# Unabsorbed prompt attention, decays of the scan by DMA, and the combine as the end of the expert stage, in one decoder layer

## The chip, the cores and the metric

The kernel runs on one core of one Trainium2 chip. The metric is the device time of one execution in microseconds. Before the change three runs gave 2944.58, 2940.27 and 2940.48, a median of 2940.48.

## The reference, cut to what matters

One decoder layer for a prompt of 512 tokens and 8 sample sequences of 8 tokens, all in float32. Three parts of it matter here.

```
# latent attention, per head h; c and kr are shared by all heads
q_lat = q_nope @ w_kv[:, h, :128].T          # 128 -> 256
s     = (q_lat @ c.T + q_rope @ kr.T) * scale, causal
o     = (softmax(s) @ c) @ w_kv[:, h, 128:]  # 256 -> 128
# chunked scan, per chunk of 128 tokens and head
a_cs     = cumsum(dt * a)
decay_ls = exp(where(causal, a_cs[l] - a_cs[s], -inf))
y_diag   = (C @ B.T * decay_ls * dt) @ x
y_off    = (C @ h_prev) * exp(a_cs);  h = exp(a_cs[-1]) * h + states
y        = rms_norm((y + D * x) * silu(z)) * g
# mixture of experts: top 4 of 32, 576 tokens
out = layer_norm(ALPHA * h + sum_k gate[t, k] * expert_k(h[t])) * g2 + b2
```

## The kernel before, in words

The program is a row of stages. Each stage is a block in which every engine has its own instruction stream, ordered by semaphores, and each ends with a barrier of all engines and a clearing of its semaphores (line 140). Inside a stage the order of work is written out by hand. A matrix product in float32 appears in the trace as two passes (two weight loads, two matmul records); a transpose is one.

`stage_prompt_attention`: 8 heads by 4 query blocks of 128 rows, 32 steps. Block q of a head sees 128(q+1) keys. Step i on TensorE: the scores of i (L402 over two halves of the 256 latent columns, L403 over the 64 rotary ones), the transposes of the probabilities of i-1 (L410), the sum over the latent rows for i-2 (L420, two halves), the value projection of i-3 (L430), and one of four parts of the preparation of the next head: its queries (L375), their absorption into the latent space in two halves (L380), its rotary queries (L386). ScalarE copies each part out (`prep_copy`), takes the exponential (L474), and copies the transposes; VectorE adds the mask (L512), takes the maximum, normalises, and copies the results (L522, L527). The next part waits for the copy of the one before; the scores of a new head wait for all four.

`stage_ssd`: 4 groups of 8 heads by 5 units (four chunks of 128 prompt tokens, and one unit of 64 sample tokens), 20 units. In loop k TensorE does `inputs(k)` (transposes, B C, and L1267, which spreads the running sum of every head over the partitions), `gate(k-1)` (L1280), the transposes of unit k-2, and `outputs(k-1)` (L1292, L1295, L1298). VectorE turns the spread sums into differences (L1490), waits for ScalarE's exponential, multiplies by B C (L1495), waits for `y_ready` of unit k-1 (L1502), and runs the chain of y, the state update and the normalisation. POOL makes three scaled copies of x (L1216). In a sample unit TensorE also turns 8 old states and multiplies them (L1317, L1326), and then makes the new states in 8 products (L1335), whose sum with the aged old ones VectorE forms (L1526) while TensorE waits for a free bank. SP loads and stores; it waits for the stores of the states before it loads the next ones. The first computation (L1429) waits for four loads, the last of which is all 2048 norm gains (`gn`).

`stage_experts` runs 32 experts in a counted loop and then up to 18 overflow items, each behind a branch (L1899), none of them taken in this execution. Each item's rows go to DRAM by an indirect DMA of POOL. `stage_combine` (SP L2147, POOL L2168 and L2170, ACT L2175, DVE L2191 to L2204) is a stage of its own: SP loads the four rows of every token for a tile of 128 tokens (three buffers of 2 MB), VectorE adds them one after another to ALPHA times h, then takes statistics and normalises, and POOL applies gain and bias.

Of the kernel before, what the change touches and what calls it, by code (L numbers as in the profile page):

```python
# [8 lines left out]
F32 = mybir.dt.float32  # L9
# [303 lines left out]
def stage_prompt_attention(nc, io, sb):  # L313

    with ExitStack() as ctx:
# [6 lines left out]
        qn_h = buf("qn_h", [P, T])  # L322
        ql_h = buf("ql_h", [P, 2, 2, SEQ])
# [3 lines left out]
        olT = buf("olT", [P, 2, 2, P])  # L327
# [9 lines left out]
        pt_ready, pt_out, pv_ready, pv_out, o_ready, o_out = (sem(n) for n in ("pt_ready", "pt_out", "pv_ready", "pv_out", "o_ready", "o_out"))  # L337
# [4 lines left out]
        with nc.Block() as block:  # L342
# [6 lines left out]
            def _(pe):  # L349
# [17 lines left out]
                def prep(h, part):  # L367
# [4 lines left out]
                    if part == 0:  # L372
                        for piece, b in ((0, 0), (1, 1)):
                            for k in range(2):
                                mm = pe.matmul(banks[:, b, 0:H2], wq[:, k, h * QH:h * QH + NOPE],  # L375
                                               sb.qnT[:, k, piece * H2:(piece + 1) * H2], start=(k == 0), stop=(k == 1))
                    elif part < 3:
                        r = part - 1
                        for piece in range(2):
                            mm = pe.matmul(banks[:, piece, 0:H2], wkT[:, h, r * P:(r + 1) * P],  # L380
                                           qn_h[:, piece * H2:(piece + 1) * H2], start=True, stop=True)
# [6 lines left out]

                pe.wait_ge(rot_out, NT)
                pe.wait_ge(wk_out, 4)  # L390
                for part in range(4):
                    prep(0, part)
                for i in range(n_steps + 3):
                    if i < n_steps:
# [6 lines left out]
                        for r in range(2):  # L401
                            pe.matmul(o, ql_h[:, h % 2, r, q * P:(q + 1) * P], sb.cT[:, r, 0:n], start=(r == 0), stop=False)  # L402
# [9 lines left out]
                    if 2 <= i <= n_steps + 1:  # L412
                        j = i - 2
                        pe.wait_ge(pt_out, j + 1)
                        if j >= 1:
                            pe.wait_ge(pv_out, j)
                        q = step(j)[1]
                        for r in range(2):
                            for k in range(q + 1):
                                mm = pe.matmul(banks[:, 5, r * P:(r + 1) * P], sb.c_tok[:, k, r * P:(r + 1) * P], probT[:, j % 2, k, :],  # L420
                                               start=(k == 0), stop=(k == q))
                        mm.then_inc(pv_ready, 1)
                    if 3 <= i:
                        j = i - 3
                        h = step(j)[0]
                        pe.wait_ge(pv_out, j + 1)
                        if j >= 1:
                            pe.wait_ge(o_out, j)
                        for r in range(2):
                            mm = pe.matmul(banks[:, 6, 0:P], sb.wkv[:, r, h * 256 + NOPE:(h + 1) * 256], olT[:, j % 2, r, :],  # L430
                                           start=(r == 0), stop=(r == 1))
                        mm.then_inc(o_ready, 1)
# [4 lines left out]
            def _(act):  # L437
                def prep_copy(h, part):
                    m = 4 * h + part
                    act.wait_ge(prep_ready, m + 1)  # L440
                    S1 = SEQ - H2
                    if part == 0:
                        act.activation(qn_h[:, 0:H2], banks[:, 0, 0:H2], ACT.Copy)
                        ins = act.activation(qn_h[:, H2:T], banks[:, 1, 0:H2], ACT.Copy)
                    elif part < 3:
                        r = part - 1
                        if h >= 2:
                            act.wait_ge(scored, 4 * h - 4)
                        act.activation(ql_h[:, h % 2, r, 0:H2], banks[:, 0, 0:H2], ACT.Copy)
                        act.activation(ql_h[:, h % 2, r, H2:SEQ], banks[:, 1, 0:S1], ACT.Copy)  # L450
                        ins = act.activation(sb.qlS[:, r, :, h, :], banks[:, 1, S1:H2].rearrange("p (b t) -> p b t", b=NSEQ), ACT.Copy)
# [4 lines left out]

                for part in range(4):
                    prep_copy(0, part)
# [21 lines left out]
            def _(dve):  # L480
# [19 lines left out]
                for i in range(n_steps + 3):  # L500
# [16 lines left out]
                    if 2 <= i <= n_steps + 1:  # L517
                        j = i - 2
                        dve.wait_ge(pv_ready, j + 1)
                        if j >= 2:  # L520
                            dve.wait_ge(o_ready, j - 1)
                        dve.tensor_copy(olT[:, j % 2, :, :], banks[:, 5, 0:2 * P].rearrange("p (r n) -> p r n", r=2)).then_inc(pv_out, 1)  # L522
                    if 3 <= i:
                        j = i - 3
                        h, q = step(j)
                        dve.wait_ge(o_ready, j + 1)
                        dve.tensor_copy(sb.oT[:, h, q * P:(q + 1) * P], banks[:, 6, 0:P]).then_inc(o_out, 1)  # L527
# [598 lines left out]
def stage_ssd(nc, io, sb):  # L1126

    with ExitStack() as ctx:
# [4 lines left out]
        gn = buf("gn", [P, DI])  # L1133
# [8 lines left out]
        dec = buf("dec", [P, 2, HG, P])  # L1142
# [10 lines left out]
        st_out = buf("st_out", [P, 4, NST])  # L1153
# [18 lines left out]
        with nc.Block() as block:  # L1172
            @block.sync
            def _(sp):
# [3 lines left out]
                for g in range(G):  # L1178
                    if g >= 2:
                        sp.wait_ge(z_ready, NT * (g - 1))  # L1180
# [47 lines left out]
            def _(pe):  # L1228
# [9 lines left out]
                def inputs(k):  # L1238
# [25 lines left out]
                    if k >= 1:  # L1264
                        pe.wait_ge(seg_out, k)
# [1073 lines left out]
```

## Time and profile before

| | us |
|---|---|
| median of 3 runs | 2940.48 |
| profiled execution, its time | 2944.55 |
| its span, first to last instruction | 2942.8 |
| prompt attention, 92.5 to 295.9 | 203.4 |
| scan, 897 to 1313 (with the stores at its end) | 416 |
| experts, 1690 to 2854 | 1164 |
| tail, 2854 to 2942.8 | 88.8 |

All times inside the execution are those of the trace, counted from its first instruction. Where a block of several records is given one duration, that is from its first start to its last end, and the ends of matmuls are modelled: blocks on TensorE overlap a little. The number in brackets behind a row is how long the engine was idle before it, and what released it.

### The profile page before, as it was taken

How to read it: one execution, taken by the hardware profiler on the slowest of the kernel's cores; microseconds unless marked ns; L12 is line 12 of the kernel's file. 1: busy time of each engine (PE TensorE's matmuls, PEld its weight loads, DVE VectorE, ACT ScalarE, POOL GpSimd, SP SyncE). 2: the span in 40 equal slices, each digit the busy share in tenths (PEclk: the TensorE clock that was granted, in tenths of full speed). 3: DMA queues.
4: the chain of work that ended last, by engine and by line, in shares of the span. 5: the costliest groups of instructions: out<-in, count | busy, mean ns of one | idle time of the engine just before them, and what ended most of it. 6: DMA issues, size and time to landing. Idle time of an engine off the chain costs nothing. (4 is left out here: it accounts for less than half of the span.)

```text
span 2942.8 us, 36532 instructions
## 1 busy us (share of the span) xinstructions
PE 2590.7 (88%) x13181; PEld 1970.4 (67%) x13181; DVE 1811.8 (62%) x2324; ACT 1345.9 (46%) x1418; POOL 480.5 (16%) x343
## 2 busy tenths in 40 slices
PE   8699899888996999979976189999999999999970
PEld 5376555588994555538843178888888888888860
DVE  0434344332775456541113389999999999999977
ACT  0233232132333444330001077777777777777750
POOL 0000222000001122100000422222222222222214
PEclk9799999988997999879988599999999999999995
DMA  2100444132213112232222199999999999999964
GB/s 85 60 1 1 183 166 166 61 86 63 87 58 106 51 43 86 61 82 66 58 104 86 21 374 403 380 381 380 378 382 379 380 381 378 382 378 379 378 234 175
DMA packets 240095, 581.16 MB, mean 197 GB/s; under 512 B 25344, under 2 KB 114496, under 8 KB 234816
## 3 DMA queue, kind: packets, MB, share of 16 engines
q1 hardware_dynamic: 221384, 503.17, 47.1%
q0 software_dynamic: 17312, 76.57, 7.0%
q8 instruction: 69, 1.13, 0.2%
q14 instruction: 34, 0.28, 0.0%
q10 hardware_dynamic: 1296, 0.01, 0.0%
HBM read 546.87 MB, written 32.71 MB: 197 GB/s over the span
## 5 line engine op out<-in xcount | busy, mean ns | idle before, releaser
L2085 DVE TENSOR_TENSOR w_lo<-w_raw,w_hi 128x2048 fp32r<-128x2048 f32 x290 | 660.5, 2296 | 67.1 <-ACT w_hi L2042 66.8
L2042 ACT ACTIVATE w_hi<-w_raw 128x2048 fp32r<-128x2048 f32 x290 | 554.3, 1916 | 108.9 <-PE banks L1986 108.8
L1986 PE MATMUL banks<-w_hi,x_hi 128*128 128x512 f32 x1024 | 319.4, 393 | 5.2 <-DVE x_lo L2089 5.2
L1986 PE MATMUL banks<-w_hi,x_lo 128*128 128x512 f32 x1024 | 316.4, 390 | 0.0
L1986 PE MATMUL banks<-w_lo,x_hi 128*128 128x512 f32 x1024 | 316.0, 390 | 0.0
L2085 DVE TENSOR_TENSOR w_lo<-mergedT,w_hi 128x2048 fp32r<-128x2048 f32 x98 | 223.6, 2288 | 46.4 <-ACT w_hi L2042 46.4
L2042 ACT ACTIVATE w_hi<-mergedT 128x2048 fp32r<-128x2048 f32 x98 | 187.6, 1915 | 98.5 <-SPq L1932 63.5
L1986 PEld LDWEIGHTS banks<-w_lo,x_hi 128*128 128x128 f32 x1024 | 192.5, 188 | 40.7
L1986 PEld LDWEIGHTS banks<-w_hi,x_lo 128*128 128x128 f32 x1024 | 192.5, 188 | 40.4
L1986 PEld LDWEIGHTS banks<-w_hi,x_hi 128*128 128x128 f32 x1024 | 190.3, 188 | 43.4 <-issue 5.6
L1958 POOL DMA_INDIRECT y_rows<-xT,to_row x33 | 50.5, 1530 | 866.3 <-ACT xT L2072 866.1
L1986 PE MATMUL banks<-w_hi,h_lo 128*128 128x512 f32 x512 | 158.2, 390 | 0.0
L1986 PE MATMUL banks<-w_lo,h_hi 128*128 128x512 f32 x512 | 158.0, 390 | 0.0
L1986 PE MATMUL banks<-w_hi,h_hi 128*128 128x512 f32 x512 | 158.0, 390 | 0.0
L1280 PE MATMUL banks<-wz,xT 128*128 128x512 f32 (+1 forms) x320 | 141.8, 596 | 0.0
L917 PE MATMUL banks_a<-xbcT,w_br_a 128*128 128x288 f32 x512 | 125.5, 406 | 0.0
L1980 PE MATMUL banks<-const,xT 128*128 128x128 f32 x520 | 68.3, 275 | 58.2 <-DMA xT<-h_rows,from_row 58.2
L917 PEld LDWEIGHTS banks_a<-xbcT,w_br_a 128*128 128x128 f32 x512 | 96.8, 190 | 26.0
L1986 PEld LDWEIGHTS banks<-w_hi,h_hi 128*128 128x128 f32 x512 | 96.1, 188 | 20.6
L1986 PEld LDWEIGHTS banks<-w_hi,h_lo 128*128 128x128 f32 x512 | 96.1, 188 | 20.3
L1986 PEld LDWEIGHTS banks<-w_lo,h_hi 128*128 128x128 f32 x512 | 96.1, 188 | 20.3
L1980 PEld LDWEIGHTS banks<-const,xT 128*128 128x128 f32 x520 | 61.5, 143 | 66.9 <-DMA xT<-h_rows,from_row 58.3
(400 smaller groups left out, 4622.7 us busy)
## 6 DMA issues: line engine op xcount, KB each, us to landing
w_raw<-in_exp_w_gu SPq DMA_DIRECT2D x194, 1024.0 KB, 7.6
w_raw<-in_exp_w_down SPq DMA_DIRECT2D x96, 1024.0 KB, 8.3
mergedT<-in_exp_w_gu SPq DMA_DIRECT2D x66, 1024.0 KB, 8.4
mergedT<-in_exp_w_down SPq DMA_DIRECT2D x32, 1024.0 KB, 5.5
w_x<-in_w_in SPq DMA_DIRECT2D x12, 1024.0 KB
out<-h SPq DMA_DIRECT2D x20, 512.0 KB
wz<-in_w_in SPq DMA_DIRECT2D x4, 2048.0 KB
h<-in_state_ssm SPq DMA_DIRECT2D x16, 512.0 KB
```

Source lines behind the costliest of these rows:

```text
L917: mm = pe.matmul(banks[:, b + 2 + piece, 0:H2], w_br[:, m % 2, k, :], x_of(k)[:, piece * H2:(piece + 1) * H2], start=(k == 0), stop=(k == ...
L1280: mm = pe.matmul(banks[0:n, 7, :], sb.xT[:, q, P * i:P * i + n], wz[:, g % 2, q, :], start=(q == 0), stop=(q == KD - 1))
L1958: pool.indirect_dma_start(out=io.y_rows, out_offset=bass.IndirectOffsetOnAxis(ap=to_row[:, par, :].bitcast(U32), axis=0), in_=y_out, in_of ...
L1980: mm = pe.transpose(banks[:, TURN_BANK[unit], k * P:(k + 1) * P], src[:, (k0 + k) * P:(k0 + k + 1) * P], K[:, K_ID:K_ID + P])
L1986: mm = pe.matmul(banks[:, bank + c, :], x[:, k, :], part[:, s % NHI, j, c * 512:(c + 1) * 512], start=start, stop=last)
L2042: act.activation(w_hi[:, s % NHI], raw(s, par), ACT.Copy).then_inc(hi_ready, 1)
L2085: dve.tensor_tensor(w_lo[:, s % NHI], raw(s, par), w_hi[:, s % NHI].bitcast(F32), ALU.subtract).then_inc(lo_ready, 1)
```

## The change

Three stages change. In attention the keys and values of the prompt are made per head (`kn_h`, `val`); the absorbed queries are made for the 64 sample tokens only. In the scan the running sums are made once, written to DRAM, and read back spread over the partitions, one DMA for each unit, into three buffers; VectorE subtracts and clamps in two instructions over all heads; the old states are aged before the new ones are ready; the norm gains are loaded group by group, last in the queue, and no computation of the first part waits for them; SP's order is written out anew. The combine becomes the end of the expert stage: rows land in buffers that the weights used, TensorE sums h and three gated rows in PSUM with diagonal matrices, VectorE adds the fourth, and gain and bias are VectorE's.

```diff
 # attention, TensorE
-            for piece in range(2):
-                mm = pe.matmul(banks[:, piece, 0:H2], wkT[:, h, r * P:(r + 1) * P], qn_h[:, piece * H2:(piece + 1) * H2], start=True, stop=True)
+        elif part == 1:
+            for r in range(2):
+                mm = pe.matmul(banks[:, 0, :], sb.wkv[:, r, h * 256:h * 256 + NOPE], sb.cT[:, r, 0:SEQ], start=(r == 0), stop=(r == 1))
+        elif part == 2:
+            for r in range(2):
+                mm = pe.matmul(banks[:, 1, r * NS:(r + 1) * NS], wkT[:, h, r * P:(r + 1) * P], qn_h[:, h % 2, SEQ:T], start=True, stop=True)
+    for u in range(8):
+        i, half = divmod(u, 2)
+        pe.wait_ge(wk_out, u + 1) if u < 4 else pe.wait_ge(val_out, u - 3)
+        for r in range(2):
+            mm = pe.matmul(banks[:, 2 + u % 4, :], sb.cT[:, r, i * P:(i + 1) * P], w_val[:, r, 4 * half:4 * half + 4], start=(r == 0), stop=(r == 1))
+    for part in range(4): prep(0, part)
-        for r in range(2):
-            pe.matmul(o, ql_h[:, h % 2, r, q * P:(q + 1) * P], sb.cT[:, r, 0:n], start=(r == 0), stop=False)
+        pe.matmul(o, qn_h[:, h % 2, q * P:(q + 1) * P], kn_h[:, h % 2, 0:n], start=True, stop=False)
         pe.matmul(o, qr_h[:, h % 2, q * P:(q + 1) * P], sb.krT[:, 0:n], start=False, stop=True).then_inc(scored, 1)
-        for r in range(2):
-            for k in range(q + 1):
-                mm = pe.matmul(banks[:, 5, r * P:(r + 1) * P], sb.c_tok[:, k, r * P:(r + 1) * P], probT[:, j % 2, k, :], ...)
+        for k in range(q + 1):
+            mm = pe.matmul(banks[:, 5 + j % 2, 0:P], val[:, k, h, :], probT[:, j % 2, k, :], start=(k == 0), stop=(k == q))
-        for r in range(2):
-            mm = pe.matmul(banks[:, 6, 0:P], sb.wkv[:, r, h * 256 + NOPE:(h + 1) * 256], olT[:, j % 2, r, :], ...)
 # scan
-    sp.dma_start(gn[:], io.gn.broadcast_to((P, DI))).then_inc(vec_in, 16)
+    def decays(k):
+        at = i * SH + g * HG
+        sp.dma_start(dec[0:n, k % 3, :, 0:n], io.acs_rows[at:at + HG, 0:n].unsqueeze(0).broadcast_to((n, HG, n))).then_inc(dec_in[k % 3], 16)
+    z_weights(0)
+    sp.wait_ge(rows_out, 1)
+    sp.dma_start(io.acs_rows[0:4 * SH, :], acsT[:, 0, :]).then_inc(rows_in, 16)
+    sp.dma_start(io.acs_rows[4 * SH:5 * SH, 0:NS], acsT[0:SH, 1, 0:NS]).then_inc(rows_in, 16)
+    sp.wait_ge(rows_in, 32)
+    for k in range(3): decays(k)
+    z_weights(1)
+    old_states(0)
+    for g in range(2): norm_gains(g)
+    for k in range(N):
+        sp.wait_ge(y_ready, k + 1)
+        if k + 3 < N: decays(k + 3)
+        if i == NT - 1:
+            new_states(g)
+            if g + 1 < G:
+                sp.wait_ge(h_out, 64 * (g + 1))
+                old_states(g + 1)
+        if i == 0 and 1 <= g < G - 1:
+            sp.wait_ge(z_ready, NT * g); z_weights(g + 1)
+            sp.wait_ge(normed, NT * g); norm_gains(g + 1)
-        for h in range(HG):
-            mm = pe.matmul(banks[0:n, 2 + h // 4, ...], dta[0:n, i, ...].broadcast_to((n, n)), tri(i, n), start=True, stop=True)
-        for h in range(HG):
-            ins = dve.tensor_scalar(dec[0:n, k % 2, h, 0:n], banks[0:n, 2 + h // 4, ...], acs[0:n, i, ...], 0.0, ALU.subtract, ALU.min)
+        dve.wait_ge(dec_in[k % 3], 16 * (k // 3 + 1))
+        dve.tensor_tensor(seg, seg, own, ALU.subtract).then_inc(seg_step, 1)
+        dve.wait_ge(seg_step, k + 1)
+        dve.tensor_scalar(seg, seg, 0.0, None, ALU.min).then_inc(seg_out, 1)
+        if i == NT - 1:
+            for b in range(NSEQ):
+                dve.wait_ge(hT_ready, NSEQ * g + b + 1)
+                dve.tensor_tensor(h0[:, :, b, :], h0[:, :, b, :], e_seq[:, :, b:b + 1].broadcast_to((P, 4, NST)), ALU.mult).then_inc(aged, 1)
-            for b in range(4):
-                ins = dve.scalar_tensor_tensor(out=h0[:, q, s, :], in0=h0[:, q, s, :], scalar=e_seq[:, q, s:s + 1], in1=banks[...], ...)
+            ins = dve.tensor_tensor(old, old, banks[:, 6 + u % 2, :], ALU.add)
 # combine, behind items() in the expert stage
+    def load(i):
+        for k in range(TOPK):
+            sp.dma_start(rows[i % 4][0:ROWS[i], k, :], src[:, k, :]).then_inc(row_in[i % 4][k], 16)
+    sp.wait_ge(y_copied, n_more + (E + 1))
+    (gain and bias are loaded)
+    sp.wait_ge(lo_ready, n_more * NW + (E + 1) * NW + AHEAD)
+    sp.wait_ge(y_stored, n_more * 16 + 16 * (E + 1))
+    for i in range(NT - 1): load(i)
+    sp.wait_ge(summed, 1)
+    load(NT - 1)
+    for i in range(NT - 1):
+        pe.wait_ge(raised, i + 1)
+        weigh(i, None)                 # identity times h, two halves of 512
+    for i in range(NT):
+        for k in range(BY_PE):         # BY_PE = 3
+            pe.wait_ge(row_in[i % 4][k], 16 * (i // 4 + 1))
+            mm = weigh(i, k)           # diag(gate) times rows
+        mm.then_inc(part_ready, 1)
+    for i in range(NT):
+        dve.wait_ge(part_ready, i + 1)
+        dve.scalar_tensor_tensor(out=x, in0=rows[i % 4][0:n, BY_PE, :], scalar=sb.gate[0:n, i, BY_PE:TOPK], in1=banks[0:n, ...], op0=ALU.mult, op1=ALU.add)
+        ...                            # statistics and normalisation as before
+        dve.tensor_tensor(x, x, g_b[0:n], ALU.mult).then_inc(gained, 1)
+        dve.tensor_tensor(x, x, b_b[0:n], ALU.add).then_inc(done, 1)
-        pool.tensor_tensor(x, x, g_b[0:ROWS[i]], ALU.mult).then_inc(scaled, 1)
-        pool.tensor_tensor(x, x, b_b[0:ROWS[i]], ALU.add).then_inc(done, 1)
```

## Rows read from the trace of the kernel before

**Rows 1.** Windows: stretch, its us, busy by engine, clock, DMA share, GB/s
```profile
core 0: us, PE busy (x) PEld busy (x) DVE busy (x) ACT busy (x) POOL busy (x), PEclk, DMA share, GB/s
975.30:1069.60 94.30, 91.65 (x395) 50.83 (x394) 51.19 (x133) 41.61 (x59) 20.11 (x17) 0.93 0.23 70
...
1006.00:1014.00 8.00, 7.96 (x10) 2.47 (x8) 4.81 (x18) 0.00 (x0) 0.00 (x0) 0.50 0.00 0
...
2854.00:2942.80 88.80, 0.00 (x0) 0.00 (x0) 55.27 (x51) 7.14 (x11) 32.11 (x11) 0.51 0.40 151
```

**Rows 2.** Groups by line on TensorE in one head, 209.82 to 230.56: busy us, mean ns
```profile
L420 PE MATMUL banks<-probT,c_tok 128*128 128x128 f32 x40 | 5.1, 275 | 0.0
L402 PE MATMUL banks<-cT,ql_h 128*128 128x128 f32 (+3 forms) x16 | 5.1, 439 | 0.8 <-ACT qrS L454 0.8
...
L430 PE MATMUL banks<-olT,wkv 128*128 128x128 f32 x16 | 2.4, 275 | 0.0
L380 PE MATMUL banks<-qn_h,wkT 128*128 128x288 f32 x8 | 2.3, 406 | 0.0
```

**Rows 3.** Timeline of TensorE at the turns of two heads: start us, us, instruction [idle before]
```profile
209.82 0.71 PE L402 MATMUL banks<-cT,ql_h 128*128 128x128 f32 x4 [0.79 <-ACT qrS L454]
...
230.56 0.71 PE L402 MATMUL banks<-cT,ql_h 128*128 128x128 f32 x4 [0.79 <-ACT qrS L454]
```

**Rows 4.** Timeline, last attention block of 512 keys: mask, then transposes
```profile
285.74 0.30 DVE L512 TENSOR_TENSOR banks<-banks,const 128x128 f32<-128x128 f32 x1 [1.59 <-PE banks L403]
...
288.54 0.66 PE L410 MATMUL banks<-const,prob 128*128 128x128 f32 x4 [1.02 <-DVE prob L507]
```

**Rows 5.** Timeline, first scores and last instruction of the attention stage
```profile
129.00 1.22 PE L402 MATMUL banks<-cT,ql_h 128*128 128x128 f32 x4 [0.79 <-ACT qrS L454]
...
294.81 0.29 DVE L527 COPY oT<-banks 128x128 f32<-128x128 f32 x1 [0.87 <-PE banks L430]
```

**Rows 6.** Timeline, two full units of the scan
```profile
934.53 0.69 DVE L1502 TENSOR_TENSOR off<-banks,e_acs 128x512 f32<-128x512 f32 x1 [4.30 <-PE banks L1295]
...
940.96 2.15 DVE L1490 TENSOR_SCALAR dec<-banks,acs 128x128 f32<-128x128 f32 x8
...
944.23 1.22 DVE L1495 TENSOR_TENSOR dec<-dec,cb 128x1024 f32<-128x1024 f32 x1 [1.12 <-ACT dec L1384]
...
947.89 0.69 DVE L1502 TENSOR_TENSOR off<-banks,e_acs 128x512 f32<-128x512 f32 x1 [2.44 <-PE banks L1295]
...
949.32 1.95 PE L1267 MATMUL banks<-const,dta 128*128 128x128 f32 x16
...
951.11 7.03 PE L1280 MATMUL banks<-wz,xT 128*128 128x512 f32 x16
```

**Rows 7.** Timeline, a sample unit's state update and the unit behind it
```profile
1000.11 0.68 DVE L1502 TENSOR_TENSOR off<-banks,e_acs 64x512 f32<-64x512 f32 x1 [14.57 <-PEq L1330]
...
1004.03 9.93 PE L1335 MATMUL banks<-b_of,xend 64*128 64x512 f32 x12 [1.95 <-DVE h L1526]
...
1015.79 3.36 PE L1267 MATMUL banks<-const,dta 128*128 128x128 f32 x16
```

**Rows 8.** Timeline, first computation of the scan
```profile
906.45 0.33 DVE L1429 TENSOR_TENSOR t<-dt,dt_b 128x160 f32<-128x160 f32 x1 [12.66 <-DMA gn<-in_ssd_norm_g]
```

**Rows 9.** Timeline of the combine: first load, tile 0, second tile, last
```profile
2869.24 0.35 SPq L2147 DMA_DIRECT2D rows<-y_rows  x1
...
2877.45 5.25 DVE L2191 SCALAR_TENSOR_TENSOR h<-rows,gate,h 128x1024 f32<-128x1024 f32 x4 [22.26 <-DMA rows<-y_rows]
...
2884.92 0.81 DVE L2204 TENSOR_SCALAR h<-h,mv 128x1024 f32<-128x1024 f32 x1
2885.65 9.15 DVE L2191 SCALAR_TENSOR_TENSOR h<-rows,gate,h 128x1024 f32<-128x1024 f32 x4
...
2936.59 2.33 POOL L2170 TENSOR_TENSOR h<-h,b_b 64x1024 f32<-64x1024 f32 x1
```

**Rows 10.** End of the expert block, by line: duration ns, first and last start us
```profile
L1912 POOLq DRAIN  x1: 5454/5454/5454, 2862.9 to 2862.9; - x1
L1912 PEldq DRAIN  x1: 8/8/8, 2863.1 to 2863.1; - x1
```

More of the change, by code:

```diff
@@ L455, in prep_copy @@
                     ins.then_inc(prep_out, 1)
+                for u in range(8):
+                    i, half = divmod(u, 2)
+                    act.wait_ge(val_ready, u + 1)
+                    act.activation(val[:, i, 4 * half:4 * half + 4, :], banks[:, 2 + u % 4, :].rearrange("p (h v) -> p h v", h=4), ACT.Copy).then_inc(val_out, 1)
                 for part in range(4):
@@ L499, in _ @@
                     dve.tensor_copy(wkT[:, 2 * u:2 * u + 2, :], banks[:, 2 + u, :].rearrange("p (h r) -> p h r", h=2)).then_inc(wk_out, 1)
-                for i in range(n_steps + 3):
+                for i in range(n_steps + 2):
                     if 1 <= i <= n_steps:
@@ new lines, in _ @@
+                z_weights(0)
[3 more added lines that the diff above has]
+                sp.wait_ge(rows_in, 32)
+                for k in range(3):
+                    decays(k)
+                z_weights(1)
+                old_states(0)
+                for g in range(2):
+                    norm_gains(g)
@@ L2032, in _, with weigh @@
                 turn(U_X1, x_raw, 4)
-                items(pe, run)
+                n_more = items(pe, run)
+                def weigh(i, k):
+                    n = ROWS[i]
+                    left, right = (K[0:n, K_ID:K_ID + n], h[0:n, i, :]) if k is None else (diag[i * BY_PE + k][0:n, 0:n], rows[i % 4][0:n, k, :])
+                    for c in range(2):
+                        mm = pe.matmul(banks[0:n, 2 * (i % 4) + c, :], left, right[:, c * 512:(c + 1) * 512], start=(k is None), stop=(k == BY_PE - 1))
+                    return mm
+                pe.wait_ge(y_copied, n_more + (E + 1))
+                pe.wait_ge(turned_lo, n_more * 4 + (4 * E + 2))
+                for i in range(NT - 1):
+                    pe.wait_ge(raised, i + 1)
+                    weigh(i, None)
+                pe.wait_ge(diag_made, 1)
+                for i in range(NT):
+                    if i == NT - 1:
+                        pe.wait_ge(raised, NT)
+                        pe.wait_ge(summed, 1)
+                        weigh(i, None)
+                    for k in range(BY_PE):
+                        pe.wait_ge(row_in[i % 4][k], 16 * (i // 4 + 1))
+                        mm = weigh(i, k)
+                    mm.then_inc(part_ready, 1)
             @block.scalar
@@ L2079, in _ @@
                 items(act, run)
+                for i in range(NT):
+                    act.activation(h[0:ROWS[i], i, :], h[0:ROWS[i], i, :], ACT.Copy, scale=ALPHA).then_inc(raised, 1)
+                for i in range(NT):
+                    n = ROWS[i]
+                    act.wait_ge(mean, 2 * i + 2)
+                    act.activation(mv[0:n, i, 1:2], mv[0:n, i, 1:2], ACT.Sqrt).then_inc(rooted, 1)
             @block.vector
@@ L2183, in _ @@
+                n_more = items(dve, run)
+                dve.wait_ge(y_copied, n_more + (E + 1))
+                dve.wait_ge(turned_lo, n_more * 4 + (4 * E + 2))
+                for i in range(NT):
+                    for k in range(BY_PE):
+                        ins = dve.tensor_scalar(diag[i * BY_PE + k], K[:, K_ID:K_ID + P], sb.gate[:, i, k:k + 1], None, ALU.mult)
+                ins.then_inc(diag_made, 1)
                 for i in range(NT):
```

251 lines of the change are left out of this document (105 added, 146 removed).

## Prediction

> **What bounds the kernel now.** I read the page first, then windows by stage, then, for each of the three stages that the diff touches, the timeline, the waits and the groups by line. The three stages are separate in time, with a barrier between each and its neighbours, so what one gains no other takes back; the sum is one of three terms.
>
> Prompt attention is a loop of eight heads that TensorE fills: a head lasts 20.74 us (209.82 to 230.56), and in it TensorE waits once, 0.79 us, for ScalarE's copy of the rotary queries [rows 3]. VectorE and ScalarE have slack, but their chain for one block of 512 keys, from the mask to the transposes, is 2.8 us (285.74 to 288.54), and at the last block TensorE waits 1.02 us of it out [rows 4].
>
> The scan runs four groups of five units, 94.3 us a group [rows 1]. In a full unit TensorE is busy throughout and VectorE is the one that waits, 2.44 us of 13.36 [rows 6]. The group's last unit ends in the update of the sample states: TensorE waits 1.95 us for VectorE, and then its clock is granted at half, so that the state products and the inputs of the next unit run at 1.2 GHz [rows 1, 7].
>
> The tail, from 2854, has no matrix product at all, and the clock stands at half [rows 1]. The combine stage doesn't begin before POOL's drain of its own DMA queue is over at 2868.4 [rows 10]; then the first rows land at 2877.45, and VectorE is the bound: four accumulations take 5.25 us on tile 0, but 9.15 us on the next tile while POOL works on the same memory [rows 9].
>
> **Attention, term by term.** Per head the change halves two blocks and drops two. The key product replaces two latent ones: half of L402's 5.1. The value product is 10 matmuls where L420 has 20: half of 5.1. L430 goes (2.4), L380's eight passes go (2.3) [rows 2]. Added are the keys of a head, two matmuls of 512 columns, four passes; L1280 runs 16 such passes in 7.03 us, 0.43 apart with 0.16 of drain [rows 6], so 1.88; and two of 64 columns for the sample queries, not over 0.6, the size of one L430 block (a quarter of 2.4). That is 9.8 less 2.5, or 7.3 in busy time. Busy time counts the drain of each block, which the next block overlaps by 0.1 to 0.16; over the ten blocks that vanish or shrink I take 1.2 off: 6.1. Then the wait at the head's turn grows. TensorE has less to do between the scores of block 3 and the end of the rotary transposes, while ScalarE copies only after its exponential, which stands behind VectorE's 2.8 us chain: 1.5 instead of 0.79. A head shrinks by 5.4 to about 15.3; seven give 38. The eighth has no preparation of a next head and is partly bound by the chain; with one pipeline step fewer in the drain that ends at 295.1 [rows 5] I take 9. Against it stand the values: eight units of two 512-column matmuls, 32 passes at 0.43, 13.7 us, ahead of the first score at 129.0 [rows 5, 6]. They start about 2 us before the preparation starts now, and the preparation behind them finds a full clock where now it has half for most of it (4 us). I take plus 8, and 1 more for small waits: minus 38. Bounds: minus 46 if no new wait appears; minus 26 if every head also waits 1.5 us at a second place.
>
> **Scan.** The eight matmuls that spread the running sums over the partitions go: L1267's block, 1.79 from start to next start in a full unit (949.32 to 951.11) [rows 6], 3.36 in the unit behind the state update, at half clock [rows 7], and about 1.0 in the 64-row unit, half the rows and columns. In their place come 20 DMAs of 0.5 MB, two units ahead, in a group whose DMA share is 0.23 [rows 1]: hidden by two units of 11.6 us. SP's queue also holds the state stores, and it waits for their landing before it goes on; but the next load of decays is needed only two units on, so this too is covered. If it were not, VectorE would be late next, and TensorE's L1292 behind it.
>
> VectorE trades eight reads of PSUM (2.15) for one subtraction of 1024 elements (the 1.22 of L1495) and one clamp (0.81 of L2204): 2.03, the same [rows 6, 9]. So its chain stays near 10.9 (13.36 less 2.44) against TensorE's 11.57, and TensorE is still the bound by 0.7. A group then loses 1.8 + 3.3 + 1.8 + 1.8 + 1.0 = 9.7; three groups 29. The state update: aging of the old states moves into the 14.57 us in which VectorE has nothing [rows 7], and TensorE waits for one addition of 512 (0.69, the size of L1502 [rows 6]) in place of four fused operations; I take minus 0.4 a group. At half clock TensorE's products set the pace (9.93 us for 12 passes [rows 7]), so the cheaper VectorE work is worth no more. The start: VectorE no longer waits 12.66 us for the 1 MB of gains [rows 8] but for three small loads, some 4 us less; then five more sums on a cold TensorE (2), a round trip of two DMAs and the first decays (about 8 before the first subtraction), and the gains, now last in the queue, hold the first normalisation some 2. With the first group's own L1267 I take minus 10. Sum: 29 + 10 + 1.6, less 2 for VectorE's lag: minus 39. Bounds: minus 28 (below) and minus 61 (clock, below).
>
> Here a port speaks against the change. In the combine the four accumulations take 5.25 alone and 9.15 beside POOL's two products of 1024 elements: 3.9 more, some 2 us for each POOL product [rows 9]. In the scan POOL's three products, of 512 elements each, run just when the new subtraction and clamp, now on SBUF, want to start. A wait for one such product each, about 1 us at half the size, makes VectorE's chain 12.4 to 12.9, over TensorE's 11.57. The Trainium skill (GPSIMD Engine Reference, Key points) says that GpSimd shares its SBUF interfaces with VectorE where the latter has two SBUF inputs or a 2-port mode; the stretched rows agree. By that rule alone the scan would gain some 10 us less than by the rows of durations. I take it that the two shorter or idle units of each group absorb most of the lag; if not, 12 units by 0.8 are 10 us.
>
> **Combine.** The barrier and the drain go from the path. SP may load once the last scatter has landed, about 2858.5 rather than 2869.2; it takes 16 DMAs of 0.5 MB, the first tile's four in the 8.2 us that the first 2 MB take now, 2869.24 to 2877.45 [rows 9], so 2867. TensorE leaves its branches at 2863.1 [rows 10] with a clock at half [rows 1]. It must stream h for four tiles first: 1.72 a tile (four 512-column passes of 0.43), 6.9 warm, 13.7 cold; I take 9.5, between the two, since it begins at half clock and would run about 5 us of it so if the clock rises as it does at the start of other stages. Three gated rows of tile 0 are 5.2: 2877.9. From there VectorE sets the pace: one accumulation 1.3, statistics to normalised 2.95 (2882.70 to 2885.65), and gain and bias, taken over from POOL, 1.22 each: 6.7 against TensorE's 5.2 [rows 6, 9]. Five tiles end at 2911.5; the last store costs what it does now, 3.9 from POOL's end (2938.92) to 2942.8 [rows 9]. End 2915.4: minus 27. Bounds: minus 31 (TensorE warm at once), nothing (below).
>
> **Sum.** 38 + 39 + 27 = 104. The profiled execution lasted 2944.55 us (span 2942.8) and would be 2840; it is 4 us over the median of the runs, 2940.48. So 2836.
>
> **Rivals.** (1) The clock survives the state update: TensorE's idle there falls from 1.95 to 1.5 us, and six products of 1.7 us become 0.86, five us a group, with 0.7 on the inputs behind: minus 22 more, 2814. For it: the shorter gap. Against: the gap is still long, and the products use 64 rows and did not win the clock back in the 8 us after [rows 1, 7]. (2) VectorE's chain bounds the scan through the shared port: plus 10, 2846. (3) The combine stays at half clock, as in all of the tail now [rows 1]: 10.3 a tile, parts ready at 2931.7, end 2942: plus 27, 2863. Against: TensorE would be continuously busy. (4) The other side: waits of VectorE's lag in each unit drop the clock in the scan loop itself, as the 1.95 us wait does. A full unit's 11.57 becomes about 23, 16 units cost 186, and the time is 3022; from nine such units on the kernel is slower. Against: new gaps are under 1 us each.
>
> **How the numbers follow.** Forecast 52% (own range 2824 to 2846), rival 1 20%, rival 2 13%, rival 3 8%, rival 4 3%, the rest 4% spread on both sides. 2806 to 2858 holds a little over eight in ten. A difference under 0.2% of the time, 6 us, is about what a measurement of this kernel can't tell from none. Faster 0.96, within 0.01, slower 0.03.
>
> **What would show it.** Right: a head of 15 to 15.5 us with one wait at its turn; values 14 us ahead of the first score; full scan units of 11.6 to 12.4; half clock behind each state update; first accumulation of the tail near 2878 on the old time scale and tiles 6.7 apart. Wrong if the first decays land late enough to hold TensorE beyond its gate product, if VectorE waits for its decays in the middle of a group, if the head waits at two places, or if the clock of the tail does not rise.

## The result, and the profile after

Four runs of the changed kernel took 2858.25 to 2863.50 us, a median of 2859.97; the kernel before, run beside it, had 2940.98. The ratio is 0.972 (95% interval 0.971 to 0.974): 81 us less, where the sum said 104 and 2836. The time lies 2 us above the upper end of the wider range (2806 to 2858) and 14 above that of the forecast's own (2824 to 2846). The profiled execution took 2858.25 us, its span is 2856.5.

The traces can be compared stage by stage, since each stage ends with a clearing of its semaphores. From one clearing to the next, prompt attention went from 203.1 to 168.0 us, the scan from 409.2 to 384.1, and the stages from the experts to the end from 1253.6 to 1227.1. The others together changed by under 1. So the three terms were 35.1, 25.1 and 26.5, against 38, 39 and 27: only the scan was missed by much. The three add up to 86.7 and not to 81, as the profiled execution of the kernel before lay 3.6 us above the median of its runs (2944.55), and that of the changed kernel 1.7 below.

Windows of the changed kernel: attention, scan, and in the scan the stretch behind the first update of the sample states (columns as in [rows 1]).

```profile
core 0: us, PE busy (x) PEld busy (x) DVE busy (x) ACT busy (x) POOL busy (x), PEclk, DMA share, GB/s
91.10:259.10 168.00, 144.55 (x604) 85.04 (x604) 68.94 (x226) 55.75 (x153) 0.00 (x0) 0.94 0.06 23
861.90:1246.00 384.10, 341.54 (x1290) 172.31 (x1290) 235.46 (x365) 169.81 (x245) 102.78 (x68) 0.90 0.31 95
966.00:975.00 9.00, 8.70 (x17) 3.94 (x16) 5.47 (x11) 1.98 (x3) 1.73 (x2) 0.50 0.22 67
```

TensorE's mean clock in the scan is 0.90. By the record of the granted clock it stood at half for 80.3 us of the stage, and for 84.9 before; in 55.6 and 59.1 of them TensorE was busy, in the rest idle (at the stage's start and end above all). The change left that nearly as it was.

**Attention** answers to [rows 3] and [rows 5]. Timeline of TensorE: the values, the first scores, and two turns of a head.

```profile
114.25 14.00 PE L398 MATMUL banks<-wkv,cT 128*128 128x512 f32 x32 [1.39 <-DVE wkT L500]
...
136.37 0.77 PE L413 MATMUL banks<-kn_h,qn_h 128*128 128x128 f32 x2 [0.88 <-ACT qrS L451]
...
167.77 0.49 PE L413 MATMUL banks<-kn_h,qn_h 128*128 128x128 f32 x2 [1.17 <-ACT qrS L451]
...
182.93 0.49 PE L413 MATMUL banks<-kn_h,qn_h 128*128 128x128 f32 x2 [1.16 <-ACT qrS L451]
```

A head lasts 15.16 us (167.77 to 182.93; foreseen about 15.3) and has one wait, at its turn. The values take 14.0.

**Scan, first computation.** Timeline of VectorE; it answers to [rows 8].

```profile
868.78 0.33 DVE L1458 TENSOR_TENSOR t<-dt,dt_b 128x160 f32<-128x160 f32 x1 [11.15 <-DMA d_b<-in_ssd_d]
```

It starts 6.9 us behind the clearing at 861.8; before, it was 8.5 us (906.45, clearing at 898.0). So 1.5 us are won here, where the sum had some 4.

**Scan, a full unit.** Timeline of VectorE, POOL, ScalarE and TensorE; it answers to [rows 6].

```profile
991.02 1.67 DVE L1517 TENSOR_TENSOR dec<-dec,acs 128x1024 f32<-128x1024 f32 x1
991.57 2.02 POOL L1244 TENSOR_TENSOR xend<-xs_t,w_end 128x512 f32<-128x512 f32 x1
992.72 1.42 DVE L1519 TENSOR_SCALAR dec<-dec 128x1024 f32<-128x1024 f32 x1
...
994.17 1.06 ACT L1413 ACTIVATE dec<-dec 128x1024 f32<-128x1024 f32 x1 [2.67 <-DVE dec L1519]
...
995.25 1.28 ACT L1421 ACT_TABLE_LOAD   x1
...
997.04 0.59 ACT L1428 ACTIVATE xbcT<-banks 128x512 f32<-128x512 f32 x1
...
997.77 0.63 PE L1280 MATMUL banks<-const,xbcT 128*128 128x128 f32 x4 [0.79 <-ACT xbcT L1428]
```

Subtraction and clamp take 3.09 us beside POOL, not 2.03. VectorE and POOL take turns: the subtraction, 1.22 us when alone (below, "POOL later"), ends 0.45 late behind a product of POOL, POOL's next one takes 2.02 instead of 1.04 as it stands through the subtraction, and then the clamp, 0.69 when alone, stands through that. Exponential, table load, silu and the copy of the transposed y follow on ScalarE, and TensorE waits for the last of them. One unit later the same row of work holds it longer: timeline of TensorE at the first old state, and of ScalarE ahead of it.

```profile
1030.88 1.06 ACT L1413 ACTIVATE dec<-dec 128x1024 f32<-128x1024 f32 x1 [2.66 <-DVE dec L1519]
1031.96 1.28 ACT L1421 ACT_TABLE_LOAD   x1
...
1033.99 1.99 PE L1343 MATMUL banks<-const,h 128*128 128x128 f32 x8 [1.84 <-ACT zs L1421]
1035.91 1.60 PE L1352 MATMUL banks<-h0T,c_of 128*64 128x512 f32 x2
```

L1352 takes 1.07 elsewhere: the clock fell to half for 3.4 us at this wait. It did so in two of the three groups that have the wait; in the first group it stayed at full. At the end of the group (answers to [rows 7]):

```profile
962.74 8.44 PE L1361 MATMUL banks<-b_of,xend 64*128 64x512 f32 x12 [1.51 <-DVE h L1557]
971.48 1.09 PE L1280 MATMUL banks<-const,xbcT 128*128 128x128 f32 x4 [0.30 <-PE banks L1361]
...
973.00 8.32 PE L1306 MATMUL banks<-wz,xT 128*128 128x512 f32 x16
```

TensorE still waits 1.51 us, the clock still falls, and as L1267 is gone from behind the update, the half clock lies on the next gate: 8.32 us instead of 7.03. The waits of TensorE over the whole scan, longest first:

```profile
PE banks L1361 <- DVE h L1557: 6.0, 4, 1.5
PE banks L1343 <- ACT zs L1421: 5.5, 3, 1.8
PE banks L1280 <- ACT xbcT L1428: 4.0, 4, 1.7
PE banks L1375 <- DVE y L1567: 3.4, 2, 2.0
PE banks L1306 <- ACT zs L1421: 1.0, 1, 1.0
```

The second, third and fifth are new: 5.5 us for ScalarE's silu, 4.0 for its copy of the transposed y, 1.0 for the silu once more. Of the fourth, 1.36 us is new too: the first normalisation waits for the gains (the other 2.0 lies under the last stores).

**Tail** (answers to [rows 9]): first load of rows, first sums, second and third tile.

```profile
2801.54 1.75 SPq L1978 DMA_DIRECT2D mergedT<-y_rows  x4
2803.26 9.72 PE L2097 MATMUL banks<-h,const 128*128 128x512 f32 x16 [12.45 <-ACT h L2162]
...
2818.18 1.28 DVE L2223 SCALAR_TENSOR_TENSOR h<-mergedT,gate,banks 128x1024 f32<-128x1024 f32 x1 [12.16 <-PE banks L2097]
...
2825.00 1.27 DVE L2223 SCALAR_TENSOR_TENSOR h<-w_raw,gate,banks 128x1024 f32<-128x1024 f32 x1
...
2831.82 1.27 DVE L2223 SCALAR_TENSOR_TENSOR h<-w_raw,gate,banks 128x1024 f32<-128x1024 f32 x1
```

The experts begin 60.0 us earlier than before. With these added, the first addition is at 2878.2 (foreseen 2877.9), the end at 2916.5 (2915.4), and tiles are 6.82 apart (6.7).

### The profile page after: what moved, and what is told of

Same layout as the page of the kernel before. It is cut to its first block and busy times, and to the rows that moved or that the text cites. A ratio compares the mean times of both kernels' runs of the same rounds, so it can differ in the third digit from the quotient of the medians.

```text
span 2856.5 us, 35192 instructions
## 1 busy us (share of the span) xinstructions
PE 2562.5 (90%) x12631; PEld 1912.8 (67%) x12631; DVE 1801.7 (63%) x2118; ACT 1344.1 (47%) x1396; POOL 472.1 (17%) x333
## 5 line engine op out<-in xcount | busy, mean ns | idle before, releaser
L1306 PEld LDWEIGHTS banks<-wz,xT 128*128 128x128 f32 (+1 forms) x320 | 57.6, 185 | 74.7 <-issue 74.3
```

Source lines behind the costliest of these rows:

```text
L1306: mm = pe.matmul(banks[0:n, 7, :], sb.xT[:, q, P * i:P * i + n], wz[:, g % 2, q, :], start=(q == 0), stop=(q == KD - 1))
```

## The experiments

The open question was the scan: is it the port beside POOL, the order on ScalarE, or the clock? Each run below edits the changed kernel unless it says otherwise. Times of whole executions are to be compared by their ratio to the kernel before, run beside them on the same chip: it had 2938.9 us beside the first four, 2936.06 beside the next four, 2943.52 beside the last three. Even so they mix in the sample attention, which no run touches: it took 293 to 294 us in the first eight runs, on two chips, and 299 to 302 in the last three, on a third.

So the scan is judged by its own stage, clearing to clearing, together with the time in it that TensorE was busy while its clock stood at half. Passes of 512 columns begin 0.43 us apart at full clock and 0.85 at half, so half of that time is what the clock cost. The last column is the stage less this half; it is an estimate. Two executions of the changed kernel, 3.4 us apart in the stage, have the same there.

| run | ratio to before | scan us | busy at half us | scan less half of it |
|---|---|---|---|---|
| before | 1 | 409.2 | 59.1 | 379.6 |
| changed kernel | 0.972 | 384.1 | 55.6 | 356.3 |
| the same again | 0.9715 | 387.5 | 62.4 | 356.3 |
| silu first | 0.969 | 384.1 | 59.4 | 354.4 |
| two states first | 0.968 | 381.9 | 50.3 | 356.8 |
| POOL later | 0.970 | 386.5 | 69.3 | 351.9 |
| eight instructions | 0.973 | 397.7 | 69.7 | 362.8 |
| all states first | 0.962 | 361.5 | 15.8 | 353.6 |
| no gaps | 0.960 | 355.9 | 9.2 | 351.3 |
| three stages | 0.970 | 390.4 | 72.3 | 354.3 |
| all edits | 0.956 | 353.9 | 9.1 | 349.4 |
| all edits, POOL later | 0.955 | 350.5 | 12.6 | 344.2 |
| before, states first | 0.9955 | 395.7 | 39.6 | 375.9 |

**Silu first.** In the loop in which the sample unit's gate ends, ScalarE does the silu ahead of the next unit's exponential.

```diff
+                    first = 1 <= k <= N and unit(k - 1)[1] == NT - 1
+                    if first:
+                        silu(k - 1)
                     act.activation(dec..., dec..., ACT.Exp).then_inc(dec_out, 1)
-                    silu(k - 1)
+                    if not first:
+                        silu(k - 1)
```

> Theory (the queue of ScalarE): in the fifth unit of each group TensorE waits 1.84 us to turn the first old state, because the gate's silu stands behind the next unit's exponential and a table load. With the silu ahead of it that wait goes; the second turn then waits for ScalarE's copy of the final state, which comes about 0.9 us earlier than now, and the short half-clock stretch behind the wait (1.0 us in three groups) goes: 4 x 0.9 + 3 x 1.0 = 6.6 us, so 2853. Rival (the port): the silu is late only since VectorE's two passes are stretched beside POOL; then the order alone gives back under 1 us, 2859 to 2860.

The 1.84 us wait went, and one of 1.34 us for the copy of the final state came one instruction later:

```profile
938.48 0.66 PE L1343 MATMUL banks<-const,h 128*128 128x128 f32 x4 [1.34 <-ACT st_out L1443]
954.14 10.61 PE L1361 MATMUL banks<-b_of,xend 64*128 64x512 f32 x12 [1.51 <-DVE h L1561]
```

The short half-clock stretch went too, but the one at the update now covers all twelve passes (10.61 us, not 8.44), and the stage is as long as it was. The ratio of 0.969 isn't this edit's work: its sample attention was 293.6 where the profiled execution of the changed kernel had 300.0. With the clock taken out the order is worth 1.9 us, where 3.6 were expected without the clock, since the wait for the final state takes back the rest.

**Two states first.** VectorE adds the first two state products ahead of the chain of y.

```diff
                         dve.tensor_tensor(off, banks[5], e_acs, ALU.mult).then_inc(y_step, 1)
+                        if i == NT - 1:
+                            add(0)
+                            add(1)
```

> VectorE adds the first two state products ahead of the chain of y, so TensorE's 1.5 us gap in the state update should go. Theory A (the gap is what lowers the clock): the gap goes (1.5 x 4), six products at full clock save about 3.3 a group and the inputs and the gate behind them 1.8: some 24 us, 2836. Theory B (the clock falls there without the gap too, as the products use 64 rows): only the gap goes, at most 6 us, 2854, and the clock is at half behind it as now.

```profile
956.74 5.26 PE L1361 MATMUL banks<-b_of,xend 64*128 64x512 f32 x8 [1.50 <-DVE h L1540]
```

Neither theory was tested: the gap stayed whole and only moved two products on (8 passes behind it, not 12). The stage is 2.2 us shorter, and with the clock taken out 0.5 longer.

**POOL later.** POOL's three copies wait for the clamp.

```diff
                     pool.wait_ge(xs_out, k + 1)
+                    pool.wait_ge(seg_out, k + 1)
```

> POOL's three scaled copies of x start only once VectorE has clamped. Theory (shared port): the subtraction falls from 1.67 to about 1.25 and the clamp from 1.42 to about 0.72, VectorE's chain is 1.1 us shorter in a full unit, TensorE's waits for the transposed y (4.0 us in all) and 1.1 of each 1.84 go, with the clock behind it: about 11 us, 2849. Rival: the contention only moves to the multiplication and the chain of y, which read two SBUF operands too, and nothing is won: 2858 to 2862.

```profile
993.30 1.22 DVE L1518 TENSOR_TENSOR dec<-dec,acs 128x1024 f32<-128x1024 f32 x1
994.55 0.69 DVE L1520 TENSOR_SCALAR dec<-dec 128x1024 f32<-128x1024 f32 x1
```

With nothing beside them the two take 1.91 us instead of 3.09, and TensorE's waits for the transposed y fell from 4.0 to 0.8. The wait for the silu did not: 6.6 instead of 5.5, and one of 1.8 for POOL's last copy is new. The stage came out 2.4 us longer, with 13.7 us more at half clock, which are worth 6.8; without them it is 4.4 shorter. The Trainium skill (GPSIMD Engine Reference, Key points) says that the shared interfaces bind for a VectorE instruction with two SBUF inputs or in a 2-port mode. The row of the subtraction, which has two such inputs, agrees (1.67 to 1.22). The clamp has one input and is held up as well (1.42 to 0.69); no row here tells in which mode it ran.

**Eight instructions.** One subtraction with clamp for each head, as before, but on the loaded sums.

```diff
-                        dve.tensor_tensor(seg, seg, own, ALU.subtract).then_inc(seg_step, 1)
-                        dve.wait_ge(seg_step, k + 1)
-                        dve.tensor_scalar(seg, seg, 0.0, None, ALU.min).then_inc(seg_out, 1)
+                        for h in range(HG):
+                            ins = dve.tensor_scalar(seg[:, h], seg[:, h], acs[..., h], 0.0, ALU.subtract, ALU.min)
+                        ins.then_inc(seg_out, 1)
```

> Subtraction and clamp in eight instructions of 128 columns on the loaded sums (one tensor operand each), one for each head. If the two-operand pass is what collides with POOL, the eight take 2.15 us or less, as they did from PSUM, instead of 3.09, and VectorE's chain is 0.9 shorter: 2849 to 2852. If the clamp form collides just as much, the eight take 3 us or more and the time is 2860 or more.

```profile
996.16 1.32 POOL L1244 TENSOR_TENSOR xdt<-xs_t,dt 128x512 f32<-128x512 f32 x1 [9.02 <-ACT xs_t L1411]
996.89 3.65 DVE L1517 TENSOR_SCALAR dec<-dec,acs 128x128 f32<-128x128 f32 x8
997.44 1.04 POOL L1244 TENSOR_TENSOR xend<-xs_t,w_end 128x512 f32<-128x512 f32 x1
998.44 1.04 POOL L1244 TENSOR_TENSOR xd<-xs_t,d_b 128x512 f32<-128x512 f32 x1
```

The eight by themselves, from the same trace (duration ns: shortest, median, longest; first and last start us):

```profile
L1517 DVE TENSOR_SCALAR dec<-dec,acs x8: 274/274/1080, 996.9 to 1000.3; 128x128 f32<-128x128 f32 x8
```

3.65 us, longer than the two, and longer than the 2.15 that the same form took from PSUM [rows 6]. But the form isn't slow: three of the eight lie beside POOL's three products and last 0.67, 1.08 and 1.08 us, each until 0.1 us behind the end of the product that was running; the five behind them take 0.27 and start 0.20 apart. So an instruction with one tensor operand waits for POOL too, and eight short ones wait three times where two long ones wait twice. TensorE's waits for the transposed y rose to 13.9 us in 11 places: here VectorE's chain plainly bounds the scan, as it lengthens by 0.56 a unit and the stage by 13.6 us, 7 of them clock.

**The changed kernel again.**

> The changed kernel without an edit, as the reference for the runs beside it. The first four runs had a sample attention stage of 293 to 294 us where the profiled execution of the changed kernel had 300, a stage that none of them touches. If that is the execution and not the kernel, this one gives about 2852 to 2860 and its scan stage 384 us again, between the clearings of semaphores before and behind it.

The sample attention was 293.3 us and the time 2852.74: it isn't the edits that make the difference. The ratio to before is 0.9715, again. The scan took 387.5, 3.4 more, with 6.8 us more at half, which are the whole of it: the same program loses a different amount to the clock each time.

**All states first.** All eight additions stand ahead of the chain of y.

```diff
+                        if i == NT - 1:
+                            for u in range(8):
+                                add(u)
```

> VectorE adds all eight state products ahead of the chain of y in the sample unit (with two of them ahead, the 1.5 us gap only moved two products on, and the scan was 2.2 us shorter). An addition is 0.69 us and a product 0.86, so TensorE has no gap there. Theory A (the gap lowers the clock): no half clock behind the update, 1.5 + 3.3 + 1.8 us a group in three groups and 1.5 to 4.8 in the last: the scan stage falls from 384 to about 362. Theory B (half clock comes from the long wait for the silu ahead of it, or from the products themselves): only the gaps go, 378 or so, with as many microseconds at half clock as now (72).

Timeline of TensorE, and the window over the update and the gate behind it:

```profile
1036.01 7.66 PE L1361 MATMUL banks<-b_of,xend 64*128 64x512 f32 x16
1043.98 0.63 PE L1280 MATMUL banks<-const,xbcT 128*128 128x128 f32 x4 [0.30 <-PE banks L1361]
```

```profile
952.90:970.00 17.10, 16.80 (x52) 7.40 (x53) 12.57 (x20) 4.43 (x7) 3.88 (x2) 1.00 0.58 169
```

Theory A. Sixteen passes run without a wait in 7.66 us, the clock stays at 1.00 through update and gate, and the scan is 361.5: 23 to 26 us shorter for an order of instructions, 20 to 23 of them clock. The same products on 64 rows run at full clock, so it wasn't they that lowered it. From update to update it is 83.1 us instead of 88.8.

**No gaps.** As well, ScalarE does silu, transposed y, final state and first old state of the sample unit ahead of the exponential.

```diff
+                            if b == 0 and k < N:
+                                decay_exp()     # behind the copy of the first old state
```

> As the run before, and in the sample unit ScalarE does silu, transposed y, final state and first old state before the exponential of the next unit, so that TensorE's 1.84 us wait goes too. If each of the two gaps brings its own stretch at half clock, both stretches of the three groups go (13.65 us a group at half, 6.8 lost) and the waits (3.3 a group): the scan stage falls from 384 to about 354. If the clock falls without gaps, it stays over 375.

355.9, 5.6 less, against 354 expected: 3.3 of it are clock (15.8 to 9.2 us at half), the rest waits. The 1.84 us wait is 0.25 now, but the exponential holds up one later copy, 1.1 us in three groups. No half clock is left behind any update; of the 9.2 us that stay 8.5 are at the start of the stage.

**Three stages.** One edit in each stage.

```diff
 # attention: rotary queries are part 2, sample queries part 3
-                        pe.wait_ge(prep_out, 4 * h + 4)
+                        pe.wait_ge(prep_out, 4 * h + 3)
 # scan, SP
+                norm_gains(0)
                 z_weights(1)
 # tail: h of tiles 0 and 1 first, h of tile i + 2 behind the rows of tile i
```

> Three edits in three places, each read from its own stage. Attention: the rotary queries are prepared in the third step of a head and the sample queries in the fourth, and the scores wait for the third: the 1.17 us wait at the turn of seven heads goes, and no other comes, if it is ScalarE's place behind the exponential that makes it: attention 8 us shorter (168 to 160). Scan: the first group's gains are loaded ahead of the second z weights and the old states: TensorE's waits of 1.36 and 2.0 us for the first two normalised units go, 3 us. Tail: h of tiles 2 and 3 is streamed behind the rows of tiles 0 and 1: the first sum is ready 3.4 us earlier if the rows have landed by then (rival: they land no earlier than they are used now, and nothing is won), but TensorE then needs 6.9 a tile where VectorE needs 6.8. Sum 11 to 14 us.

```profile
151.09 0.66 PE L421 MATMUL banks<-const,prob 128*128 128x128 f32 x4 [0.82 <-DVE prob L508]
```

Attention took 160.8, 6.1 less than the same kernel without the edit, not 8: behind the wait for ScalarE stands one of 0.82 us for VectorE's chain, so a head is 0.34 us shorter (14.83 instead of 15.17), not 1.17. Most of the 6.1 is the first head, 4.4 us shorter, in which a stretch of 6.8 us at half clock is gone. In the tail the first addition came 13.96 us behind the first load of rows instead of 16.64, and the last stages took 1224.4 instead of 1227.2: 2.9 of 3.4. In the scan TensorE's wait for the gains is gone, 1.36 us, but with 9.9 us more at half than its twin the stage is 2.9 longer; corrected for the clock it is 2.0 shorter.

**All edits, and POOL later with them.** The edits of the runs "no gaps" and "three stages", and values ahead of transposes in attention; then POOL's wait on top.

> The edits of the two scan runs and of the run with three stages together, and one more: in a head TensorE multiplies the values of the block before last ahead of the transposes of the last block, so that 0.83 us of work lies where it now waits 0.82 us for the probabilities at each head's turn. The three edited stages were 355.9 (scan), 160.8 (attention) and 2.7 us less at the end. If the gains add: scan 353 (first gains 3 us), attention 155, and 2853 - 35 - 3 - 12 - 3 = 2800. If the transposes, now later, hold up ScalarE's copies, attention stays at 160 and the time is 2806.

> As the run before, with POOL's three copies behind VectorE's clamp. With POOL later the clamp and the subtraction took 1.91 instead of 3.09, and TensorE's waits for the transposed y fell from 4.0 to 0.8 us, but 6.8 us more were lost at half clock. Theory (shared port, and the clock no longer in the way): the scan stage is 3 to 5 us shorter than in the run before. Rival: TensorE then waits for POOL's third copy instead (1.8 us once), and the chain of y is slower beside POOL: no difference.

All edits: 2813.60 us (2813.16 to 2816.06), ratio 0.956 (0.955 to 0.958). Attention 159.1: a head is 14.35 us instead of 15.17, not the 14.0 expected. Scan 353.9, end 1225.0. With POOL later: 2810.14 us (2806.08 to 2813.52), ratio 0.955 (0.954 to 0.957). The whole times don't part the two, their stages do: 350.5 for the scan, with 3.5 us more at half, so 5.2 us for the port, now that the clock is out of the way. It beats both kernels, the changed one by 1.7%.

**Before, with all states first.**

> The kernel before the change with one edit: VectorE updates the sample states (its fused form, four instructions for a product) ahead of the chain of y. If the 1.95 us gap is what lowers the clock there too, its scan stage, 409.2, falls by 1.95 + 5 + 1.8 a group or somewhat less, as four fused instructions for a product take 1.0 us against 0.86 of TensorE: 20 to 28 us, so about 2911 to 2916. The scan stage against the 361.5 of the changed kernel with the same edit then gives what the change itself is worth in the scan with the clock out of the way: 1.8 us a full unit, 0.6 to 1 in the others, and the start, 28 us, if the terms of the sum hold and no wait takes them back. If the clock falls without a gap, the time is 2930 or more.

```profile
995.17 2.16 PE L1335 MATMUL banks<-b_of,xend 64*128 64x512 f32 x4 [0.36 <-DVE h L1510]
996.21 0.29 PEld L1335 LDWEIGHTS banks<-b_of,xend 64*128 64x128 f32 x2 [0.74 <-DVE h L1510]
997.51 7.19 PE L1335 MATMUL banks<-b_of,xend 64*128 64x512 f32 x8 [0.18 <-DVE h L1510]
```

Half of what was expected: 395.7. Four fused instructions take 1.12 us for a product of 0.86, TensorE waits several times for 0.18 to 0.36 us, and the clock still fell, behind these. With the old states aged ahead of time an addition takes 0.69 us, less than a product, and the gaps are gone: that is the difference between the two kernels at this place, though no run changed it alone. The sum valued it at 0.4 us a group. Between the two kernels with this edit, 395.7 and 361.5, lie 34 us; less the difference in clock, (39.6 - 15.8) / 2, they are 22.3, where 28 was expected.

## Why the prediction was wrong

**Attention, right.** 35.1 measured, 38 foreseen. Head, its single wait (1.16, foreseen 1.5), values and first score (7.4 us later than before in the trace, 8.6 behind the stage's own start) are as the terms had them. The remaining 3 us are the first head, in which the pipeline fills: it was 18.6 us (129.00 to 147.58) and is 16.2 (136.37 to 152.59), 2.4 less and not 5.4 like the others. The last head with its drain gave 7.9 of the 9, the six between 5.6 each. The clock moves this term too: in the run "before, states first" the unchanged attention stage took 199.2 us instead of 203.1.

**Combine, right.** 26.5 against 27, with the first addition within 0.3 us, though the rows were loaded 3 us later than forecast: the streaming of h, not the rows, holds the first tile. The clock did rise, and rival 3 did not come.

**Scan, the step that failed.** The sum's 39 came out as 25. The failed sentence is "TensorE is still the bound by 0.7", with "the two shorter or idle units of each group absorb most of the lag". From the twelve passes of one update to those of the next it was 94.8, 95.0 and 93.3 us, and is 88.8, 88.8 and 85.0 (the last group has no exponential ahead of its silu, and no such wait): 20.4 us instead of 3 x 10.1. Of the 10 for the start and the first group 5.1 came (the passes of the first update began 106.0 us behind the clearing, and begin 100.9 behind it). By cause:

- New waits of TensorE, 11.9 us: 5.5 for the silu, 4.0 for the transposed y, 1.0 for the silu of the second unit, 1.36 for the gains. The sum had 2 for the lag and some 2 for the gains, and a wait of 1.5 us of before went. That is 6 to 7 us too little.
- A part of it is the port, rival 2's mechanism, which the text priced at 10 and gave 13%. It acts in 13 of the 16 full units (3.09 us against 1.91), and as the text had it: VectorE stands until a product of POOL is over. Taking it away gave 4.4 us once and 5.2 once (both after correction for the clock). The edit with eight instructions shows the same bound from the other side.
- The rest is ScalarE, which no term or rival had: in a loop it holds an exponential, a silu and a square root with three table loads of 1.28 us, in an order that was harmless while TensorE had 1.8 us of L1267 ahead of each gate. The wait for the silu stayed when the port was freed, and went when the order changed.
- The clock. The sum credited L1267 behind the update with 3.3 us, its price at half clock, where 1.8 is its price at full: 4.5 us over three groups. But the half clock lasts nearly as long without it (59.1 and 55.6 us, worth 1.8) and falls on the next gate: 2.7 us too much.

Waits and clock make 9 of the missing 14. Another 2.5 are the first computation, which came 1.5 us earlier behind the clearing and not some 4, as the load of D held it up. The 10 for the start and the first group was estimated from no row of a like start; what it lacks is this and the first group's share of the new waits, 5.9 us of the 11.9, against 2 foreseen and 1.5 gone. The other 2 of the 14 are spread over the later groups and stay open.

**Rival 1** (the clock survives the update) was refused with the right reason, the gap; by the changed order it came true and was worth 23 to 26 us, waits included (priced at 22). Rival 4 came in a small form only: single waits of 1.8 us lowered the clock for 3.4 us, in two of three groups. The range missed on its upper side because the scan alone left its bound (28 promised as the least, 25 came), and that bound knew only one way for the lag to come. That the median lies just outside and not just inside is chance: 104 less the 17 us by which the three terms were short gives 2854, inside the wider range, and the rest is how far the two profiled executions lay from the medians of their runs.

## What to carry to other kernels

A wait on TensorE ahead of a stretch of work costs more than its length: 1.5 us of idle time brought 5 to 6 us more a group at half clock, and letting VectorE free TensorE's banks first removed both. When a bound engine loses work, write down what every other engine does in one period in its order, table loads included, and price what is taken out of a half-clock stretch at full clock, as the stretch moves on to what follows. Where VectorE and POOL both work in SBUF, add POOL's product to VectorE's chain for each instruction that can meet one. Judge an edit by its stage and by the time at half clock in it, not by the whole time: silu first and POOL later saved 1.9 and 4.4 us of waiting and left the stage as long as it was, or longer, until the clock was settled.

## What the runs showed of the hardware that was not expected

- Waits of 0.18 to 0.36 us between products, two or three a group, stood ahead of each fall of the clock behind an update in the kernel before with its states first; without any, sixteen passes on 64 rows and the gate behind them ran at full clock.
- The same kernel was busy at half clock for 55.6 and 62.4 us of its scan in two executions; the stage less half of that was 356.3 us both times.
- In SBUF, VectorE and POOL took turns by whole instructions: three subtractions with clamp of 128 columns lasted 0.67, 1.08 and 1.08 us, to the end of POOL's product each, and the next five 0.27, starting 0.20 apart. From PSUM eight of them took 2.15 us, 0.26 apart.
- ScalarE's table load takes 1.28 us, and the activation starts right behind it (1031.96 and 1033.26). The Trainium skill (ScalarE: Activation LUTs, What ACT_TABLE_LOAD costs) gives the same 1283 ns and adds a drain of about 1380 ns to each switch; no row here shows such a drain ahead of an activation.
- A stage that no run touched, the sample attention, took 293.0 to 294.0 us in eight runs on two chips and 299.2 to 301.6 in three on a third.
